# Two memory-key chunks inside the compression, and GpSimd in place of VectorE for the recurrence's resets

## The chip, the cores and the metric

One core of a Trainium2 chip runs the whole kernel. The metric is the device time of one execution in microseconds; lower is better. TensorE (PE), VectorE (DVE), ScalarE (ACT) and GpSimd (POOL) run their own instruction lists and meet only at semaphores; SyncE (SP) issues the weight transfers.

## The reference, cut to what matters

A decoder trunk of two layers over 512 tokens of width 1024. Layer 0 mixes with pooled channels and sparse attention, layer 1 with a gated linear recurrence (RG-LRU). Each layer then does cross-attention into 256 memory tokens and a gated FFN, with a layer norm after each part. The two pieces that the change touches:

```
# layer 0, sparse attention: 32 x 64 inputs of a block are compressed to one key and one value
blocks = raw[:, idx] + pos_emb[None, None, :, None, :]      # 31 blocks of 32 tokens
kc = rotary(blocks @ cmp_wk) ; vc = blocks @ cmp_wv
# layer 0, cross-attention: keys of the memory
kv = mem @ wkv ; k = kv[..., :D]
# layer 1, recurrence over the tokens, 1280 channels in 10 blocks of 128
r = sigmoid(xb @ wa + ba) ; i = sigmoid(xb @ wx + bx)
log_a = -8 * r * softplus(-lam)
a = exp(log_a) ; mult = sqrt(-expm1(2 * log_a))
reset = (positions == 0)
a = where(reset, 0, a) ; mult = where(reset, 1, mult)
h = scan(a, mult * (i * xc)) ; y = h * gelu(gate) ; out = y @ w_out
```

## The kernel before, in words

**Matrix products.** Every large product is done in three passes on TensorE: each operand is split into a rounded high part and a low remainder, and hi*hi, hi*lo and lo*hi are summed in PSUM (`passes`, L660). Weights come in chunks of 128 rows by 512 columns, through a ring of four buffers (`RING = 4`). A chunk c goes through four queues in this order:

1. SP issues the transfer into `w_raw`, once GpSimd has split chunk c-4 (`w_split`).
2. ACT rounds it into `w_hi` (`round_chunk`, L1111), once the transfer has landed and TensorE is done with chunk c-4 (`w_used`).
3. GpSimd subtracts to get `w_lo` (`split`, L623) and counts up `w_split`.
4. TensorE waits for `w_split` of chunk c, uses it, and counts up `w_used`.

GpSimd does nothing else after its first transfers: its list is `split` from the first chunk to the last, in order. Each engine's list is written out by hand. `PLAN` names groups of products, with their number of chunks and how many evacuations of PSUM ACT and DVE do for each. From it come the counts for which the engines wait (`ACT_BEFORE`, `DVE_AFTER` and so on), and the PSUM half: group i uses banks 0 to 3 or 4 to 7 in turn, and must wait for the evacuation of group i-2 (`begin`).

**Around the compression (layer 0).** TensorE does `tk` (transposes of the keys), then `cmp`: 128 small matmuls, a loop over 32 positions `l`, which the profile counts as 256 (L820). Then come chunks 0 to 3 of `k0_1` (memory keys, 8 chunks, 12 matmuls of 256 columns in each), `tkc` (transposes of the compressed keys), chunk 4, the compressed scores (L842, L845), chunk 5, `scores(0)` and `scores(1)`, chunks 6 and 7, `scores(2)`. `k0_1` lies in banks 4 to 7. The attention loop that follows transposes probabilities into banks 4 and 5 (`turn_probs`), sums outputs in bank 6 and memory values in bank 7, so it starts with `evacuated("k0_1")`: four copies by ACT (`keys_evac`, L1142), which stand behind `exps(0)`, `exps(1)` and three rounded chunks.

**The recurrence (layer 1).** The 10 channel blocks come in three sets, n = 0, 1, 2, of 4, 4 and 2. TensorE's order is `oin0`, `oin1`, the gates of set 0 (`ra0`, `ia0`; L967), `oin2`, the gates of set 1, `oin3`, the gates of set 2 (`ra2` holds both), `oin4`, then `oout0` and `oout1`. `oin4` reuses the banks of `oin3`, bank by bank, as ACT's gelu of `oin3` frees them. For each set ACT and DVE do in turn: sigmoid of r into `RA` (ACT, L1334), sigmoid of i (ACT, L1341), reset (DVE, L1758), tanh (ACT, L1350), two exponentials (ACT, L1354, L1356), `multipliers_squared` (DVE, L1786, L1788), square root (ACT, L1366), product and scan (`recurrence`, DVE, L1796, L1797), product with gelu (`y_tile`, DVE, L1804), rounding (`y_rounded`, ACT, L1304) and remainder (`y_low`, DVE). `conv` (DVE, L1768, L1771) makes the gates' input. ACT's rounding of weights is placed among these with `round_on(n, name)`. The reset works on r: `far` is 1e32 where the position is 0 and 0 elsewhere, so the maximum of r and `far` makes the decay 0 there.

Of the kernel before, what the change touches and what calls it, by code (L numbers as in the profile page):

```python
# [34 lines left out]
ALU = mybir.AluOpType  # L35
# [79 lines left out]
def plan_groups():  # L115


    g = [("x0", 0, 4, 4), ("x1", 0, 4, 4)]
    g += [("ein0", KT, 4, 0), ("tm", 0, 4, 4), ("ein1", KT, 4, 0), ("ein2", KT, 4, 0), ("ein3", KT, 4, 0)]
    g += [("mix", 0, 4, 4), ("k0_0", KT, 4, 0), ("tq0", 0, 2, 2), ("tq1", 0, 2, 2), ("tk", 0, 4, 4), ("cmp", 0, 2 + GROUP, 0), ("k0_1", KT, 4, 0), ("tkc", 0, 0, 0)]  # L120
    g += [(f"fv_{n}", KT, 1, 0) for n in range(D // FILL)]
    g += [("attn", 0, 0, 0)]
    g += [("eout0", KT, 0, 4), ("eout1", KT, 0, 4)]
    def norm(l, i, fillers=(None, None)):

        groups = [(f"ln{l}{i}_0", 0, 4, 4), (f"ln{l}{i}_1", 0, 4, 4)]
        return groups + [f for f in fillers if f]

    for l in range(DEPTH):
        if l:  # L130
            g += [("oin0", KT, 4, 0), ("oin1", KT, 4, 0), ("ra0", 0, 4, 0), ("ia0", 0, 4, 0)]
            g += [("oin2", KT, 4, 0), ("ra1", 0, 4, 0), ("ia1", 0, 4, 0)]
            g += [("oin3", KT, 4, 0), ("ra2", 0, 4, 0), ("oin4", KT, 4, 0)]
            g += [("oout0", RT, 0, 4), ("oout1", RT, 0, 4)]
            g += norm(1, 0)
        else:
            g += norm(0, 0)
        g += [(f"q{l}_0", KT, 4, 4), (f"q{l}_1", KT, 4, 4)]
        g += [(f"xo{l}_0", 0, 4, 4), (f"xo{l}_1", 0, 4, 4)]
        g += [(f"wo{l}_0", KT, 0, 4), (f"wo{l}_1", KT, 0, 4)]  # L140
        g += norm(l, 1) if l else norm(0, 1, (("k1_0", KT, 4, 0), ("k1_1", KT, 4, 0)))
        g += [(f"up{l}_{n}", KT, 2, 2) for n in range(FT // 2)]
        g += [(f"dn{l}_0", FT, 0, 4), (f"dn{l}_1", FT, 0, 4)]
        if l == 0:
            g += norm(0, 2, (("v1_0", KT, 2, 0), ("v1_1", KT, 2, 0)))
    return g
# [65 lines left out]
def hybrid_trunk(nc, a, out):  # L212

    ctx = ExitStack()
    with ctx:
# [149 lines left out]
        kc_ready = sem("kc_ready")  # L365
        scored, maxed, exped, turned = sem("scored"), sem("maxed"), sem("exped"), sem("turned")
        vc_cleared, cmp_scored, cmp_copied = sem("vc_cleared"), sem("cmp_scored"), sem("cmp_copied")
        weighted, copied_d, copied_a = sem("weighted"), sem("copied_d"), sem("copied_a")
        pv_done, o_hi_ready, o_ready = sem("pv_done"), sem("o_hi_ready"), sem("o_ready")

# [237 lines left out]
        @block.gpsimd  # L608
        def _(pool):

            for half in (0, 1):
                pool.dma_start(rows_posk[:, half, :], a["e_cmp_pos_k"][0]).then_inc(s_rows, 16)
                pool.dma_start(rows_posv[:, half, :], a["e_cmp_pos_v"][0]).then_inc(s_rows, 16)
            pool.dma_start(rows_ps[:, :], a["e_pool_scale"][0].rearrange("(g p) -> g p", p=P)).then_inc(s_rows, 16)
            pool.dma_start(rows_rg[0:CONV * RT, :], a["o_conv_w"][0].rearrange("n (j p) -> (n j) p", p=P)).then_inc(s_rows, 16)
            for n, name in enumerate(("o_conv_b", "o_ba", "o_bx", "o_lambda")):
                pool.dma_start(rows_rg[(CONV + n) * RT:(CONV + n + 1) * RT, :],
                               a[name][0].rearrange("(j p) -> j p", p=P)).then_inc(s_rows, 16)
            def split(first, last, m=0):
                for c in range(first, last):  # L620
                    (hi, lo), n = w_pair(c), WIDTH[c]
                    pool.wait_ge(w_rounded, c + 1 + RING * m)
                    nc.gpsimd.tensor_tensor(lo[:, :n], w_raw[:, c % RING, :n], hi[:, :n].bitcast(F32),  # L623
                                            ALU.subtract).then_inc(w_split, 1)

            done = 0
            for l in range(DEPTH):
                first, last = CHUNK0[f"up{l}_{UP_FIRST}"], CHUNK0[f"dn{l}_1"] + FT - HELD
                last = first + (last - first) // RING * RING
                split(done, first)  # L630
                with pool.Fori(0, (last - first) // RING) as m:
                    split(first, first + RING, m)
                done = last
            split(done, len(CHUNKS))


# [2 lines left out]
        def _(pe):  # L639
# [173 lines left out]
            pe.wait_ge(rawpos_ready, 4)  # L813
            pe.wait_ge(s_cmpw, 64)
            for l in range(CMP_BLOCK):
                for n in (0, 1):
                    for g in range(KV_HEADS):
                        half = slice(g * HD, (g + 1) * HD)
                        src = raw_pos[half, n, l // CMP_STRIDE, l:l + (NCMP - 1) * CMP_STRIDE + 1:CMP_STRIDE]
                        nc.tensor.matmul(ps[32 * n:32 * n + NCMP, b0 + g, 0:HD], src, cmp_w[half, n, l, :],  # L820
                                         start=(l == 0), stop=(l == CMP_BLOCK - 1))
            for t in range(TT):
                last = turn(ps[:, b0 + 2, t * GATES:(t + 1) * GATES], gateT[:, t * P:(t + 1) * P], GATES)
            last.then_inc(filled, 1)
            product("k0_1", mem, MEM, True, chunks=(0, KT // 2))
            b0 = begin("tkc")
            pe.wait_ge(kcdup_ready, 1)
            for g in range(KV_HEADS):
# [103 lines left out]
            product("k0_1", mem, MEM, True, chunks=(KT // 2 + 2, KT))  # L932
            pe.wait_ge(exped, 1)
            scores(2)
            evacuated("k0_1")
            for u in range(len(UNITS)):
                turn_probs(u)
                if u + 3 < len(UNITS):
                    pe.wait_ge(exped, u + 2)
                    scores(u + 3)  # L940
                for i in range(filled_until(u - 1), filled_until(u)):
                    memory_values(i)
                if u == len(UNITS) - 1:
                    evacuated("mix")
                    product("eout0", fm, SEQ, False, chunks=(0, 1), begun=True)
                weigh(u)
# [148 lines left out]
        def _(act):  # L1095
# [88 lines left out]
            filled_by("tk")  # L1184
            for j in range(4):
                nc.scalar.activation(kT_hi[:, j // 2, j % 2, :], bank("tk", j), ACT.Copy).then_inc(evac_a, 1)
            filled_by("cmp")
            b0 = 4 * (INDEX["cmp"] % 2)
            nc.scalar.activation(kc_tok[:, :, :], ps[0:NCMP, b0:b0 + 2, 0:HD], ACT.Copy).then_inc(evac_a, 1)
            act.wait_ge(vc_cleared, 2)  # L1190
# [34 lines left out]
            nc.scalar.activation(cmp_scores[:, 1, :], ps[:, 3, :], ACT.Copy).then_inc(cmp_copied, 1)  # L1225
            exps(0)
            exps(1)
            keys_evac(0, 1)
            for u in range(len(UNITS)):
                if UNITS[u][1] == "cmp" and u:  # L1230
                    output_hi(UNITS[u][0] - 1)
# [53 lines left out]
            for l in range(DEPTH):  # L1285
                if l:
# [74 lines left out]
                    def multipliers(n, meanwhile):  # L1361
                        done = sum(s[1] for s in RG_SETS[:n])
                        for j in range(RG_SETS[n][1]):
                            round_on(1 + (j == 0), meanwhile)
                            act.wait_ge(m2_ready, done + j + 1)
                            nc.scalar.activation(tm[:, j, :], tm[:, j, :], ACT.Sqrt).then_inc(mult_ready, 1)  # L1366


                    x_evac(0)
# [13 lines left out]
                    y_rounded(2, "oout0")  # L1383
                norm(l, 0)
                act.wait_ge(evac_a, ACT_BEFORE[f"q{l}_0"])
                for i in range(8):
                    if i < 4:
                        hi, full = k_hi[:, 2 * i:2 * i + 2, :], k_mem[:, 2 * i:2 * i + 2, :]
                    else:
                        m, n = (i - 4) // 2, i % 2  # L1390
                        hi, full = v_hi[:, m, 512 * n:512 * (n + 1)], v_mem[:, m, 512 * n:512 * (n + 1)]
                    nc.scalar.activation(hi, full, ACT.Copy).then_inc(kv_hi_ready, 1)
# [80 lines left out]
        def _(dve):  # L1473
# [186 lines left out]
            row_max(0)  # L1660
            row_max(1)
            weigh_probs(0)
            row_max(2)
            for u in range(len(UNITS)):
                turned_half(u)
# [71 lines left out]
            for l in range(DEPTH):  # L1737
# [5 lines left out]
                if l:  # L1743
# [5 lines left out]
                    dve.wait_ge(s_posb, 16)  # L1749

                    settle(nc.vector.tensor_copy(far[:, :], posb[:, :]))
                    settle(nc.vector.tensor_scalar(far[:, :], far[:, :], 0.0, FAR, ALU.is_equal, ALU.mult))

                    def resets(n):

                        for j in range(RG_SETS[n][1]):
                            dve.wait_ge(evac_a, ACT_BEFORE[f"ra{n}"] + j + 1)
                            nc.vector.tensor_tensor(RA[n][:, j, :], RA[n][:, j, :], far[:, :], ALU.max).then_inc(ra_reset, 1)  # L1758

                    def conv(n, part=None):  # L1760
                        first, tiles, name, b = RG_SETS[n]
# [49 lines left out]

                    conv(0)
                    conv(1, (0, 1))
                    resets(0)
                    conv(1, (2, 3))
                    multipliers_squared(0)
                    recurrence(0)
                    y_tile(0, 0)
                    y_tile(0, 1)
                    conv(2)  # L1820
                    resets(1)
                    multipliers_squared(1)
                    y_low(0, 0)
                    y_low(0, 1)
                    recurrence(1)
                    for j in range(4):
                        y_tile(1, j)
                    resets(2)
                    multipliers_squared(2)
                    for j in range(4):  # L1830
                        y_low(1, j)
                    y_tile(2, 2)
                    y_tile(2, 3)
                    recurrence(2)
                    y_low(2, 2)
                    y_tile(2, 0)
                    y_low(2, 3)
# [129 lines left out]
```

## Time and profile before

| what | value |
|---|---|
| median of 3 runs | 1492.19 us (1491.9 to 1496.13) |
| the profiled execution: its time, its span | 1492.09 us, 1490.3 us |
| PE / PE weight load busy | 98% / 82% |
| DVE / ACT / POOL busy | 38% / 41% / 45% |
| granted TensorE clock, mean | 0.999 of full speed |

The span runs from the first to the last instruction. The engines' shares are averages over the whole kernel, and the stages differ: between 855 and 960 us, where the recurrence is, DVE is busy for 90.31 of 105 us. A matmul of 512 columns is shown as 0.39 us long, but two of them start 0.23 us apart, since they overlap; idle time of PE is therefore read from the gaps that the timeline prints and not from busy shares alone.

### The profile page before, as it was taken

Reading aid. Unit: us, or ns where it says so; the run is one execution under the profiler, and the core shown is the slowest. Engines: PE = TensorE matmul, PEld = TensorE weight load, DVE = VectorE, ACT = ScalarE, POOL = GpSimd, SP = SyncE. Lnnn points to the kernel's source line nnn. Section 1 sums busy time; section 2 is a strip of 40 time slices with the busy share of each in tenths; the row PEclk is TensorE's granted clock in tenths of the full one; section 3 lists DMA queues with packets and bytes.
Section 4 is the critical chain, followed back from the end, with each engine's and each line's share of the span. In section 5 each row is a group of like instructions: output and inputs, shape, how many; then the busy total and the mean of one; then the engine's idle time right before and its main releaser. Section 6 shows DMA issues by size and latency. Waiting matters only on the chain.

```text
span 1490.3 us, 21214 instructions
## 1 busy us (share of the span) xinstructions
PE 1465.9 (98%) x7750; PEld 1227.7 (82%) x7750; DVE 559.5 (38%) x946; ACT 607.6 (41%) x1226; POOL 668.7 (45%) x530
## 2 busy tenths in 40 slices
PE   8999999999999999999999999999999999999998
PEld 7888888888888888888888867788888888888886
DVE  2753883833741101110123498664443101101014
ACT  3346764344343323332234397635433323323221
POOL 5543225233464454444457534543153454444442
PEclk9999999999999999999999999999999999999999
DMA  9332114221253333332234413323133333233222
GB/s 246 96 92 63 48 50 148 72 85 57 92 170 93 92 106 94 96 99 98 94 106 135 141 56 96 107 95 99 36 113 103 96 99 96 87 106 99 94 98 92
DMA packets 115713, 147.04 MB, mean 99 GB/s; under 512 B 20534, under 2 KB 74160, under 8 KB 115632
## 3 DMA queue, kind: packets, MB, share of 16 engines
q1 hardware_dynamic: 115312, 145.87, 32.2%
q8 instruction: 52, 0.85, 0.2%
q14 instruction: 29, 0.24, 0.1%
q0 software_dynamic: 320, 0.08, 0.0%
HBM read 143.80 MB, written 2.10 MB: 98 GB/s over the span
## 4 chain that ended last, share of the span: by engine, by line
PE 89%; DVE 4%; ACT 3%; issue 1%; POOL 1%; DMA 1%; SPq 0%; DVEq 0%; ACTq 0%
PE ps L660 81%; PE ps L665 4%; PE ps L914 1%; PE ps L868 1%; DVE h L1797 1%; POOL w_lo L623 1%; DVE h L1804 1%; DMA x_res<-in_x 1%; ACT w_hi L1111 0%; PE ps L967 0%; DVE h L1771 0%; ACT probs L1204 0%; ACT tm L1350 0%; DVE ib_alt L1788 0%; DVE ib L1796 0%
## 5 line engine op out<-in xcount | busy, mean ns | idle before, releaser
L623 POOL TENSOR_TENSOR w_lo<-w_raw,w_hi 128x512 fp32r<-128x512 f32 (+2 forms) x468 | 603.0, 1298 | 792.7 <-ACT w_hi L1111 791.0
L1111 ACT ACTIVATE w_hi<-w_raw 128x512 fp32r<-128x512 f32 (+2 forms) x468 | 279.6, 612 | 543.0 <-PE ps L660 521.7
L660 PE MATMUL ps<-fm_hi,w_hi 128*128 128x512 f32 (+1 forms) x1112 | 421.6, 379 | 4.1 <-POOL w_lo L623 3.0
L660 PE MATMUL ps<-fm_hi,w_lo 128*128 128x512 f32 (+1 forms) x1112 | 419.2, 377 | 0.0
L660 PE MATMUL ps<-fm_lo,w_hi 128*128 128x512 f32 (+1 forms) x1112 | 419.1, 377 | 0.0
L660 PEld LDWEIGHTS ps<-fm_hi,w_hi 128*128 128x128 f32 x1112 | 209.2, 188 | 45.8 <-POOL w_lo L623 4.6
L660 PEld LDWEIGHTS ps<-fm_hi,w_lo 128*128 128x128 f32 x1112 | 209.2, 188 | 38.6
L660 PEld LDWEIGHTS ps<-fm_lo,w_hi 128*128 128x128 f32 x1112 | 209.3, 188 | 38.1 <-issue 0.5
L1935 DVE TENSOR_TENSOR gf<-silu,ps 128x512 f32<-128x512 f32 x44 | 28.4, 685 | 418.8 <-ACT silu L1450 401.5
L1679 DVE SCALAR_TENSOR_TENSOR x_res<-x_res,ps 128x512 f32<-128x512 f32 x48 | 31.4, 685 | 273.5 <-PE ps L660 188.2
L660 PE MATMUL ps<-w_hi,g_hi 128*128 128x512 f32 x288 | 112.0, 389 | 0.0
L660 PE MATMUL ps<-w_hi,g_lo 128*128 128x512 f32 x288 | 112.0, 389 | 0.0
L660 PE MATMUL ps<-w_lo,g_hi 128*128 128x512 f32 x288 | 112.0, 389 | 0.0
L660 PEld LDWEIGHTS ps<-w_lo,g_hi 128*128 128x128 f32 x288 | 54.1, 188 | 11.3
L660 PEld LDWEIGHTS ps<-w_hi,g_lo 128*128 128x128 f32 x288 | 54.1, 188 | 11.2
L660 PEld LDWEIGHTS ps<-w_hi,g_hi 128*128 128x128 f32 x288 | 54.1, 188 | 11.1
L660 PE MATMUL ps<-w_hi,fm_hi 128*128 128x512 f32 x160 | 62.6, 391 | 0.4 <-ACT pool_in L1154 0.4
L660 PE MATMUL ps<-w_hi,fm_lo 128*128 128x512 f32 x160 | 62.3, 389 | 0.0
L660 PE MATMUL ps<-w_lo,fm_hi 128*128 128x512 f32 x160 | 62.3, 389 | 0.0
L1483 DVE TENSOR_TENSOR fm_lo<-ps,fm_hi 128x512 fp32r<-128x512 f32 x68 | 43.5, 684 | 23.7 <-ACT fm_hi L1137 13.7
L1263 ACT ACTIVATE lnc<-lnc 128x1 f32<-128x1 f32 x24 | 4.9, 204 | 94.8 <-DVE lnc L1719 94.8
L1137 ACT ACTIVATE fm_hi<-ps 128x512 fp32r<-128x512 f32 x48 | 26.1, 596 | 42.0 <-PE ps L665 41.6
(284 smaller groups left out, 2148.1 us busy)
## 6 DMA issues: line engine op xcount, KB each, us to landing
w_raw<-in_f_w_up SPq DMA_DIRECT2D x352, 128.0 KB, 2.1
w_raw<-in_f_w_down SPq DMA_DIRECT2D x88, 256.0 KB, 2.6
w_raw<-in_x_wkv SPq DMA_DIRECT2D x48, 256.0 KB, 3.1
w_raw<-in_o_w_in SPq DMA_DIRECT2D x40, 256.0 KB, 2.6
w_raw<-in_x_wq SPq DMA_DIRECT2D x32, 256.0 KB, 2.7
w_raw<-in_x_wo SPq DMA_DIRECT2D x32, 256.0 KB, 2.7
w_raw<-in_e_w_in SPq DMA_DIRECT2D x24, 256.0 KB, 3.3
w_raw<-in_o_w_out SPq DMA_DIRECT2D x20, 256.0 KB, 2.7
```

Of the source, the lines that this page charges most:

```text
L623: nc.gpsimd.tensor_tensor(lo[:, :n], w_raw[:, c % RING, :n], hi[:, :n].bitcast(F32), ALU.subtract).then_inc(w_split, 1)
L660: last = nc.tensor.matmul(outp, lhsT, rhs, start=(clear and k == 0 and n == 0), stop=(k == steps - 1 and n == 2), skip_group_check=True)
L665: return nc.tensor.transpose(out_, in_, ident[0:n, 0:n])
L868: last = nc.tensor.matmul(ps[:, b0 + hh % 2, c0:c0 + w], qT[:, hh, qb * P:(qb + 1) * P], k_[:, BRANCHES.index(b), hh // GROUP, :w], start= ...
L914: last = nc.tensor.matmul(quarter(ps[half, 6, cols]), kv_tok[:, kb, c0:c0 + HD], probsT[:, u % 2, turned_blocks, :], start=False, stop=(b ...
L1111: nc.scalar.activation(w_pair(c)[0][:, :n], w_raw[:, s, :n], ACT.Copy).then_inc(w_rounded, 1)
L1137: nc.scalar.activation(fm_target(hi, name, j), quarter(bank(name, j)), ACT.Copy).then_inc(evac_a, 1)
L1483: nc.vector.tensor_tensor(lo, full, hi.bitcast(F32), ALU.subtract).then_inc(done, 1)
L1679: nc.vector.scalar_tensor_tensor(out=xs, in0=xs, scalar=ALPHA, in1=bank(name, t), op0=ALU.mult, op1=ALU.add).then_inc(evac_d, 1)
L1797: nc.vector.tensor_tensor_scan(h[:, first + j, :], a_, i_, 0.0, ALU.mult, ALU.add).then_inc(h_ready, 1)
L1804: nc.vector.tensor_tensor(hj, hj, gelu[:, first + j, :], ALU.mult).then_inc(y_full, 1)
L1935: nc.vector.tensor_tensor(gf[:, j, :], silu[:, j, :], bank(name, 2 + j), ALU.mult).then_inc(evac_d, 1)
```

## The change

- `k0_1` begins inside the compression: its chunks 0 and 1 stand before position l = 24 of 32, chunks 2 and 3 after the compression.
- `k0_1` is evacuated by ACT (tiles 2, 3) and DVE (tiles 0, 1). TensorE waits only for DVE's two before the first `turn_probs`, and for ACT's two after it. ACT rounds two chunks of `k0_1` before it waits for `cmp`, and takes one of its three memory-value chunks before its copies, two after.
- The resets go from DVE to GpSimd, with add in place of maximum. GpSimd does the four, four and two of them after it has split the first chunk of `oin2`, `oin3` and `oin4`, each after a wait for ACT's sigmoid of that tile.
- In sets 1 and 2 ACT takes each square root ahead of the chunks that it rounds with it. In set 2 DVE does `recurrence(2)` ahead of `y_tile(2, 2)` and `y_tile(2, 3)`.

```diff
-... ("cmp", 0, 2 + GROUP, 0), ("k0_1", KT, 4, 0), ("tkc", 0, 0, 0)]
+... ("cmp", 0, 2 + GROUP, 0), ("k0_1", KT, 2, 2), ("tkc", 0, 0, 0)]
@@ gpsimd
                 done = last
+                if l == 0:
+                    for n, after in enumerate(("oin2", "oin3", "oin4")):
+                        split(done, CHUNK0[after] + 1)
+                        done = CHUNK0[after] + 1
+                        pool.wait_ge(far_ready, 1)
+                        for j in range(RG_SETS[n][1]):
+                            pool.wait_ge(evac_a, ACT_BEFORE[f"ra{n}"] + j + 1)
+                            nc.gpsimd.tensor_tensor(RA[n][:, j, :], RA[n][:, j, :], far[:, :], ALU.add).then_inc(ra_reset, 1)
             split(done, len(CHUNKS))
@@ tensor
             for l in range(CMP_BLOCK):
+                if l == 3 * CMP_BLOCK // 4:
+                    product("k0_1", mem, MEM, True, chunks=(0, 2))
...
-            product("k0_1", mem, MEM, True, chunks=(0, KT // 2))
+            product("k0_1", mem, MEM, True, chunks=(2, KT // 2))
...
-            evacuated("k0_1")
+            pe.wait_ge(evac_d, DVE_AFTER["k0_1"])
             for u in range(len(UNITS)):
                 turn_probs(u)
                 if u + 3 < len(UNITS):
                     pe.wait_ge(exped, u + 2)
                     scores(u + 3)
+                if u == 0:
+                    pe.wait_ge(evac_a, ACT_AFTER["k0_1"])
@@ scalar
-            filled_by("cmp")
+            round_weights(CHUNK0["k0_1"] + RING + 1)
+            group_filled(act, "cmp")
...
-            keys_evac(0, 1)
+            group_filled(act, "k0_1")
+            round_weights(CHUNK0["fv_0"] + 1)
+            for j in (2, 3):
+                nc.scalar.activation(k_mem[:, 4 + j, :], bank("k0_1", j)[:, :MEM], ACT.Copy).then_inc(evac_a, 1)
+            round_weights(CHUNK0["fv_0"] + RING - 1)
...
                         for j in range(RG_SETS[n][1]):
-                            round_on(1 + (j == 0), meanwhile)
+                            if n == 0:
+                                round_on(1 + (j == 0), meanwhile)
                             act.wait_ge(m2_ready, done + j + 1)
                             nc.scalar.activation(tm[:, j, :], tm[:, j, :], ACT.Sqrt).then_inc(mult_ready, 1)
+                            if n:
+                                round_on(1 + (j == 0), meanwhile)
@@ vector
             weigh_probs(0)
+            group_filled(dve, "k0_1")
+            for j in (0, 1):
+                nc.vector.tensor_copy(k_mem[:, 4 + j, :], bank("k0_1", j)[:, :MEM]).then_inc(evac_d, 1)
             row_max(2)
...
-                    def resets(n):
-
-                        for j in range(RG_SETS[n][1]):
-                            dve.wait_ge(evac_a, ACT_BEFORE[f"ra{n}"] + j + 1)
-                            nc.vector.tensor_tensor(RA[n][:, j, :], RA[n][:, j, :], far[:, :], ALU.max).then_inc(ra_reset, 1)
...
                     conv(1, (0, 1))
-                    resets(0)
                     conv(1, (2, 3))
...
-                    resets(1)
                     multipliers_squared(1)
...
-                    resets(2)
                     multipliers_squared(2)
                     for j in range(4):
                         y_low(1, j)
+                    recurrence(2)
                     y_tile(2, 2)
                     y_tile(2, 3)
-                    recurrence(2)
```

## Rows read from the trace of the kernel before

**Rows 1.** The page: busy shares, and the chain that ended last by engine.

```profile
PE 1465.9 (98%) x7750; PEld 1227.7 (82%) x7750; DVE 559.5 (38%) x946; ACT 607.6 (41%) x1226; POOL 668.7 (45%) x530
...
PE 89%; DVE 4%; ACT 3%; issue 1%; POOL 1%; DMA 1%; SPq 0%; DVEq 0%; ACTq 0%
```

**Rows 2.** Waits of PE, whole span: total us, times, longest us.

```profile
PE ps L660 <- POOL w_lo L623: 5.4, 9, 1.3
PE ps L820 <- issue: 1.6, 1, 1.6
PE ps L665 <- ACT k_mem L1142: 1.2, 1, 1.2
```

**Rows 3.** Window of the recurrence: length, busy PE, PEld, DVE, ACT, POOL.

```profile
855.00:960.00 105.00, 100.82 (x404) 75.23 (x403) 90.31 (x92) 84.59 (x131) 45.07 (x29) 1.00 0.27 81
```

**Rows 4.** Timeline of PE, recurrence: start, us, line, operation, [idle before, releaser].

```profile
864.09 0.79 PE L660 MATMUL ps<-fm_hi,w_hi 128*128 128x512 f32 x1
...
878.13 0.50 PE L660 MATMUL ps<-fm_hi,w_hi 128*128 128x512 f32 x1 [0.55 <-POOL w_lo L623]
...
893.58 0.79 PE L660 MATMUL ps<-fm_hi,w_hi 128*128 128x512 f32 x1
...
920.33 0.47 PE L660 MATMUL ps<-fm_hi,w_hi 128*128 128x512 f32 x1 [0.98 <-ACT gelu L1297]
...
935.35 0.50 PE L660 MATMUL ps<-fm_hi,w_hi 128*128 128x512 f32 x1 [1.13 <-POOL w_lo L623]
...
938.60 0.50 PE L660 MATMUL ps<-fm_hi,w_hi 128*128 128x512 f32 x1 [0.24 <-POOL w_lo L623]
...
959.21 0.50 PE L660 MATMUL ps<-w_hi,y_hi 128*128 128x512 f32 x1 [1.27 <-POOL w_lo L623]
```

**Rows 5.** Timeline of PE, compression and the start of the attention loop.

```profile
118.44 3.84 PE L820 MATMUL ps<-cmp_w,raw_pos 64*31 64x64 f32 x244
123.92 0.45 PE L820 MATMUL ps<-cmp_w,raw_pos 64*31 64x64 f32 x12 [1.64 <-issue]
...
148.69 0.39 PE L863 MATMUL ps<-causal_b,ident_b 128*128 128x256 bf16 x2 [0.19 <-ACT probs L1204]
```

**Rows 6.** Timeline of DVE, keys' remainder (evacuation of tk) and row_max(2).

```profile
119.18 2.48 DVE L1483 TENSOR_TENSOR kT_lo<-ps,kT_hi 128x512 fp32r<-128x512 f32 x4 [1.09 <-ACT kT_hi L1186]
...
143.95 1.22 DVE L1620 TENSOR_REDUCE negmax<-ps 128x8 f32<-128x1024 f32 x1 [2.78 <-PE ps L868]
```

**Rows 7.** Timeline of ACT, first operation of exps(2).

```profile
145.73 0.36 ACT L1204 ACTIVATE probs<-ps,negmax 128x128 f32<-128x128 f32 x1
```

**Rows 8.** Timeline of POOL, recurrence: one split, then merged runs of four and three.

```profile
853.15 1.29 POOL L623 TENSOR_TENSOR w_lo<-w_raw,w_hi 128x512 fp32r<-128x512 f32 x1 [1.19 <-ACT w_hi L1111]
...
888.51 7.02 POOL L623 TENSOR_TENSOR w_lo<-w_raw,w_hi 128x512 fp32r<-128x512 f32 x4 [10.43 <-ACT w_hi L1111]
...
913.81 5.01 POOL L623 TENSOR_TENSOR w_lo<-w_raw,w_hi 128x512 fp32r<-128x512 f32 x3 [2.70 <-ACT w_hi L1111]
```

**Rows 9.** Timeline of ACT, recurrence: one rounded chunk, and the sigmoids of r.

```profile
852.44 0.63 ACT L1111 ACTIVATE w_hi<-w_raw 128x512 fp32r<-128x512 f32 x1 [2.09 <-PE ps L660]
...
861.26 2.42 ACT L1334 ACTIVATE ra<-ps,chan 128x512 f32<-128x512 f32 x4
...
890.78 2.42 ACT L1334 ACTIVATE ra_alt<-ps,chan 128x512 f32<-128x512 f32 x4
...
922.97 1.27 ACT L1334 ACTIVATE ra<-ps,chan 128x512 f32<-128x512 f32 x2
```

**Rows 10.** Timeline of DVE: resets, and the same operation with and without POOL beside it.

```profile
864.15 3.59 DVE L1758 TENSOR_TENSOR ra<-ra,far 128x512 f32<-128x512 f32 x4
...
891.11 3.25 DVE L1804 TENSOR_TENSOR h<-h,gelu 128x512 f32<-128x512 f32 x2
...
947.86 1.29 DVE L1804 TENSOR_TENSOR h<-h,gelu 128x512 f32<-128x512 f32 x2 [0.75 <-ACT gelu L1297]
```

**Rows 11.** The page, DMA issues: KB each, us to landing.

```profile
w_raw<-in_o_w_in SPq DMA_DIRECT2D x40, 256.0 KB, 2.6
```

More of the change, by code:

```diff
@@ L119, in plan_groups @@
     g += [("ein0", KT, 4, 0), ("tm", 0, 4, 4), ("ein1", KT, 4, 0), ("ein2", KT, 4, 0), ("ein3", KT, 4, 0)]
-    g += [("mix", 0, 4, 4), ("k0_0", KT, 4, 0), ("tq0", 0, 2, 2), ("tq1", 0, 2, 2), ("tk", 0, 4, 4), ("cmp", 0, 2 + GROUP, 0), ("k0_1", KT, 4, 0), ("tkc", 0, 0, 0)]
+    g += [("mix", 0, 4, 4), ("k0_0", KT, 4, 0), ("tq0", 0, 2, 2), ("tq1", 0, 2, 2), ("tk", 0, 4, 4), ("cmp", 0, 2 + GROUP, 0), ("k0_1", KT, 2, 2), ("tkc", 0, 0, 0)]
     g += [(f"fv_{n}", KT, 1, 0) for n in range(D // FILL)]
@@ L367, in hybrid_trunk @@
         vc_cleared, cmp_scored, cmp_copied = sem("vc_cleared"), sem("cmp_scored"), sem("cmp_copied")
+        far_ready = sem("far_ready")
         weighted, copied_d, copied_a = sem("weighted"), sem("copied_d"), sem("copied_a")
@@ L1385, in _ @@
                 act.wait_ge(evac_a, ACT_BEFORE[f"q{l}_0"])
+                if l == 0:
+                    act.wait_ge(evac_d, DVE_AFTER["k0_1"])
                 for i in range(8):
@@ L1751, in _ @@
                     settle(nc.vector.tensor_copy(far[:, :], posb[:, :]))
-                    settle(nc.vector.tensor_scalar(far[:, :], far[:, :], 0.0, FAR, ALU.is_equal, ALU.mult))
-                    def resets(n):
-                        for j in range(RG_SETS[n][1]):
-                            dve.wait_ge(evac_a, ACT_BEFORE[f"ra{n}"] + j + 1)
-                            nc.vector.tensor_tensor(RA[n][:, j, :], RA[n][:, j, :], far[:, :], ALU.max).then_inc(ra_reset, 1)
+                    nc.vector.tensor_scalar(far[:, :], far[:, :], 0.0, FAR, ALU.is_equal, ALU.mult).then_inc(far_ready, 1)
                     def conv(n, part=None):
```

## The prediction

> **What bounds the kernel now.** I read the page first: PE is busy for 98% of the span and 89% of the chain that ended last is PE's [rows 1], so time is won or lost only where PE stands still. The waits of PE name those places: its waits for GpSimd's `w_lo` sum to 5.4 us over the whole kernel, one gap of 1.6 us in the compression is put down to "issue" (nothing that the profile shows), and one of 1.2 us is for the copies of `k_mem` [rows 2]. The window of the recurrence shows DVE busy for 90.31 and ACT for 84.59 of 105 us, and PE for 100.82 [rows 3]: DVE is crowded there, yet PE hardly waits. The timeline of PE shows what is to be had in that stage. Counting a gap as the distance of two starts less the usual 0.23 us, the printed idle times of 0.55, 1.13, 0.24 and 1.27 us are stalls of 0.7, 1.3, 0.4 and 1.4 us: 3.8 us together [rows 4]. No more can be won in the recurrence, however light DVE becomes. What matters instead is GpSimd: each 512-column chunk passes through it, and chunk 1 of `oin2` was split from 853.15 us, long before TensorE began `oin2` at 864.09 [rows 4, 8]. That lead is what the change spends.
>
> **The compression.** 244 of the 256 matmuls take 3.84 us (15.7 ns each), then comes the gap of 1.64 us, then the last 12 [rows 5]. The engine has its data, so I take the gap for instructions that don't arrive as fast as such small matmuls use them. The two chunks put in at l = 24 are 24 matmuls in about 2.9 us (0.12 us each); during them instructions can arrive, and the gap should go. l = 24 is reached after 192 matmuls, at 118.44 + 3.0 = 121.5; there `begin` now waits for the evacuation of `tk`, which DVE ends at 119.18 + 2.48 = 121.66 [rows 5, 6]: 0.2 to 0.3 us. Net gain 1.4 us. Chunks 0 and 1 of `k0_1` are split by then: ACT rounds up to chunk 2 of it before it evacuates `k0_0`. ACT's new rounds before `cmp` lie in 4 us in which it only waited.
>
> **The evacuation of k0_1.** PE waited 1.17 us for ACT's four copies. Now it needs two copies by DVE, which is idle for 2.78 us before `row_max(2)` [rows 6]; about 0.4 us each, they are hidden. But the wait doesn't vanish whole. `row_max(2)` needs `scores(2)`, so it still ends at 143.95 + 1.22 = 145.17, and `exps(2)`, which began at 145.73, can begin at 145.2 at best [rows 6, 7]. PE already waits 0.19 us for those exps at 148.69 [rows 5]. So some 0.5 us of the 1.2 stay as gain, between bounds of 0 and 1.2; without DVE's idle time the two copies would add 0.8 us to `row_max(2)`. This part and the last: 1.4 + 0.5 = 1.9 us gained, bounds 0 (the gap only moves) and 2.8.
>
> **The resets on GpSimd.** A reset is the same shape as a split, three 128x512 tiles in SBUF; alone a split takes 1.29 us [rows 8]. Beside a busy DVE it takes more: runs of four in 7.02 and three in 5.01 us are 1.75 and 1.67 each [rows 8]. DVE pays too: two `y_tile` products take 3.25 us with GpSimd beside them and 1.29 without, 1.0 us more each [rows 10]. DVE is busy at all three places, so I take 1.7 us, with 1.29 as the lower bound. Queued behind the resets on GpSimd are the splits, PE waits for those, and GpSimd can't start the resets before ACT's sigmoid, whatever lead it had. PE takes 2.72 us per chunk (ACT's rounding, released by PE, shows 2.09 idle + 0.63 [rows 9]); the first matmul after gates adds 0.4.
>
> - Set 0. First sigmoid done at 861.26 + 0.6 = 861.9 [rows 9]. Four resets and the split of chunk 1 of `oin2` are five operations: 861.9 + 8.5 = 870.4. PE wants that chunk at 864.09 + 0.4 + 2.72 = 867.2 [rows 4]. Stall 3.2 us (1.1 at 1.29).
> - Set 1. Sigmoid done at 891.4 [rows 9], chunk 1 of `oin3` split at 899.9, wanted at 893.58 + 3.1 = 896.7 [rows 4]. Stall 3.2 us (1.1). Sigmoid and PE are both later by then, by the same amount, as the gelus ahead of the sigmoid wait for PE's `oin2`.
> - Set 2. Sigmoid done at 922.97 + 0.65 = 923.6 [rows 9], two resets and a split, 5.1 us, chunk 1 of `oin4` at 928.7; wanted at 920.33 + 0.1 + 2.72 = 923.1 [rows 4]. Stall 5.6 us (4.4). Here even free resets would leave a stall, since the sigmoid comes too late.
>
> Sum 12.0 us (6.6). Transfers follow `w_split` too: chunk 5's is issued only when chunk 1 is split and lands 2.6 us later [rows 11], and ACT can round chunk 5 only when PE has used chunk 1, 2.7 us after the split. The two come together, so the transfer adds nothing, but ACT, and with it exps, roots and scans, now falls behind PE's delay; I count no second stall from it, as PE reaches chunk 5 another 8 us later. What a late PE takes back are the old stalls, whose causes (late rounds and late y tiles) had PE on time: 3.8 us. Net 12.0 - 3.8 = 8.2 us (2.8 at 1.29; 12.0 if none is given back).
>
> DVE loses its resets (3.59 us for the first four [rows 10]) but shares with ten resets and some three more splits at 1.0 us each: about even, and nobody waits for it in this stage once PE is late. ACT's roots ahead of rounds and `recurrence(2)` ahead of two y tiles bring results of DVE and ACT forward by 1 to 3 us, for a PE that comes 8 us late: cost and gain nothing; with PE on time they would be part of the 3.8.
>
> The Trainium skill (SBUF — State Buffer, section on who interferes with whom) says that a VectorE operation with two inputs in SBUF and a GpSimd operation that reads SBUF exclude each other for the whole instruction. By that, each reset could wait for a whole DVE operation, 1.9 us rather than the 1.7 of the rows, and the three stalls would be 15 us instead of 12.
>
> **The sum.** +8.2 - 1.9 = +6.3 us on the profiled execution's 1492.09, which is 0.1 below the median: 1498.5 us, slower by 0.42%.
>
> **Rivals.**
>
> - Within 0.3%: the resets run at 1.3 to 1.45 us, since DVE's convolution leaves GpSimd gaps. Net +2.8 to +4.5 in the recurrence, less 1.9: 1493 to 1495.5. For it: a lone split beside an idle DVE is 1.29. Against it: both long runs. 20%.
> - Faster: DVE is the real bound of the recurrence, its relief removes all old stalls, and no new one comes. 3.8 + 1.9 gives 1486.5 us. It needs five GpSimd operations between 861.9 and 867.2 us, under 1.06 each, and no row shows less than 1.29; in set 2 it can't be. 5%.
> - The clock falls: PE stands still for over 5 us in set 2. The granted clock was 1.00 throughout the stage [rows 3], with no gap beyond 1.3 us, so nothing before says what such a gap does. At 1.2 instead of 2.4 GHz a chunk takes 5.4 us; one to two such chunks add 2.7 to 5.4 us: 1501 to 1504. 12%.
> - The issue gap only moves to another place in the compression: 1500. 10%, part of the slower side.
>
> The Trainium skill (TensorE: Matmul & The Clock Gate, section on why this matters for kernels) warns that the clock drops to its lower level after idle gaps between matmuls; by it the third rival would be the likeliest for the longest gap. The waits before are too short to test it.
>
> **Numbers.** The forecast as it stands has 53%, which with the third and fourth rival makes 75% slower; 20% same, 5% faster. A difference under 0.3% (4.5 us) is what a measurement can't tell from none. Range: down to the low pace, up to the clock rival, 1493.5 to 1503.5.
>
> **What the profile after would show.** PE waits for POOL at chunk 1 of `oin2`, `oin3` and `oin4`, three gaps of about 3, 3 and 5.5 us, and none at `oout0`; resets on POOL at 1.5 to 1.8 us each; PE late by about 8 us at `oout0` less 2 us from the attention; compression without the 1.64 us gap; `turn_probs(0)` directly behind `scores(2)`. The prediction fails if chunk 1 is split in time after all, or if the three gaps feed further ones through ACT's rounds.

## The result, and the profile after

The changed kernel takes 1500.48 us (median of 4 runs, 1500.28 to 1502.19); the kernel before, timed beside it, 1492.05 us (1491.22 to 1496.13). The ratio is 1.0055, with a 95% interval of 1.0043 to 1.0067: 0.55% slower. The profiled execution took 1502.19 us, the slowest of the four; its span is 1500.4 us, 10.1 more than before.

The page and the waits of PE over the whole span of the changed kernel (times as in [rows 2]: total, count, longest):

```profile
PE 1472.5 (98%) x7750; PEld 1232.3 (82%) x7750; DVE 558.6 (37%) x938; ACT 607.8 (41%) x1224; POOL 683.8 (46%) x540
...
PE 93%; ACT 3%; POOL 2%; issue 1%; DVE 1%; DMA 0%; SPq 0%; DVEq 0%; ACTq 0%; POOLq 0%
```

```profile
PE ps L669 <- POOL w_lo L624: 11.9, 8, 3.6
PE ps L674 <- DMA x_res<-in_x: 5.3, 2, 5.0
PE ps L831 <- issue: 1.2, 1, 1.2
```

GpSimd's share rises by one point, and nothing but PE looks busy on the page; but PE's waits for `w_lo` have grown from 5.4 us [rows 2] to 11.9. The wait for `k_mem` is gone, the "issue" gap is not. DVE's part of the chain has shrunk from 4% [rows 1] to 1%: DVE was relieved, and the kernel is slower all the same.

The timeline of PE in the recurrence, to be read against [rows 4]:

```profile
868.49 0.80 PE L669 MATMUL ps<-fm_hi,w_hi 128*128 128x512 f32 x1 [2.96 <-POOL w_lo L624]
869.09 0.63 PE L669 MATMUL ps<-fm_lo,w_hi 128*128 128x512 f32 x1
869.51 0.63 PE L669 MATMUL ps<-fm_hi,w_lo 128*128 128x512 f32 x1
869.94 0.63 PE L669 MATMUL ps<-fm_hi,w_hi 128*128 128x512 f32 x1
...
882.41 0.50 PE L669 MATMUL ps<-fm_hi,w_hi 128*128 128x512 f32 x1 [0.55 <-POOL w_lo L624]
...
904.33 0.50 PE L669 MATMUL ps<-fm_hi,w_hi 128*128 128x512 f32 x1 [3.19 <-POOL w_lo L624]
...
935.06 0.50 PE L669 MATMUL ps<-fm_hi,w_hi 128*128 128x512 f32 x1 [3.62 <-POOL w_lo L624]
```

Three gaps stand at chunk 1 of `oin2`, `oin3` and `oin4`. By the distance of two starts less 0.23 us they are stalls of 3.1, 3.3 and 3.8 us. And behind the first one the matmuls start 0.43 us apart, not 0.23. The windows show why; the eighth value is the granted clock:

```profile
840.00:868.00 28.00, 25.54 (x98) 17.97 (x96) 20.24 (x18) 15.39 (x26) 18.05 (x11) 1.00 0.19 56
868.00:875.00 7.00, 6.51 (x16) 5.14 (x17) 6.86 (x6) 1.60 (x4) 5.43 (x5) 0.53 0.50 135
875.00:904.00 29.00, 25.60 (x98) 17.84 (x96) 24.73 (x25) 26.72 (x41) 14.33 (x9) 1.00 0.14 41
904.00:909.00 5.00, 4.67 (x13) 3.69 (x14) 0.00 (x0) 0.32 (x1) 3.98 (x4) 0.66 0.52 152
909.00:935.00 26.00, 22.44 (x92) 16.91 (x90) 22.24 (x22) 23.60 (x36) 10.11 (x8) 1.00 0.17 52
935.00:939.60 4.60, 4.54 (x13) 3.60 (x14) 0.56 (x1) 0.00 (x0) 4.18 (x4) 0.63 0.50 137
```

Around each gap the clock falls from 2.4 to 1.2 GHz. Counting matmuls that start 0.43 us apart, each 0.2 us late, gives 2.8, 1.5 and 1.5 us: 5.8 us in all. The first fall, with 14 such matmuls, is the odd one: the others have 8. In the profile of the recurrence part alone (below) all three falls are short, with 7 or 8 slow matmuls each.

The other side of the gaps is in GpSimd's timeline, next to [rows 8]:

```profile
860.25 6.52 POOL L642 TENSOR_TENSOR ra<-ra,far 128x512 f32<-128x512 f32 x4 [9.77 <-ACT ra L1352]
866.73 6.51 POOL L624 TENSOR_TENSOR w_lo<-w_raw,w_hi 128x512 fp32r<-128x512 f32 x4
...
895.88 6.72 POOL L642 TENSOR_TENSOR ra_alt<-ra_alt,far 128x512 f32<-128x512 f32 x4 [1.48 <-ACT ra_alt L1352]
902.55 5.43 POOL L624 TENSOR_TENSOR w_lo<-w_raw,w_hi 128x512 fp32r<-128x512 f32 x4
...
930.37 2.96 POOL L642 TENSOR_TENSOR ra<-ra,far 128x512 f32<-128x512 f32 x2 [9.85 <-ACT ra L1352]
```

GpSimd stands idle for 9.8 us at the head of its list, waiting for the first sigmoid, then does four resets in 6.5 us, and only then splits chunk 1, which needed nothing of all that.

The gates of set 0 start here, before and after:

```profile
857.62 7.03 PE L967 MATMUL ps<-h,w_gates 128*128 128x512 f32 x16
```

```profile
855.78 7.03 PE L980 MATMUL ps<-h,w_gates 128*128 128x512 f32 x16
```

The balance from there (1.84 us earlier than before) to the end of the span (10.1 later) is 11.9 us. The stalls are 10.2 and the half clock 5.8, together 16.0; given back are the old stalls of 1.3, 0.4 and 1.4 us and, with the wait for the gelu [rows 4], 1.2 us between the gates of set 2 and the second matmul of `oin4`: 4.3 together. The 0.7 us stall came back (at 882.41). 16.0 - 4.3 = 11.7. Of the 1.84 us ahead of the gates only 0.6 were won between the compression and the first scores of the attention loop; 0.3 lie ahead of 100 us and 1.1 between 410 and 425 us, around a wait of 0.64 us for `w_lo` at 420.11 that no edit touches and that most of the other profiles lack, too.

### The profile page after: what moved, and what is told of

Its sections match the earlier page's. It is cut to its first block, busy times and chain, and to the rows that moved or that the text cites. A ratio compares the mean times of both kernels' runs of the same rounds, so it can differ in the third digit from the quotient of the medians.

```text
span 1500.4 us, 21218 instructions
## 1 busy us (share of the span) xinstructions
PE 1472.5 (98%) x7750; PEld 1232.3 (82%) x7750; DVE 558.6 (37%) x938; ACT 607.8 (41%) x1224; POOL 683.8 (46%) x540
## 4 chain that ended last, share of the span: by engine, by line
PE 93%; ACT 3%; POOL 2%; issue 1%; DVE 1%; DMA 0%; SPq 0%; DVEq 0%; ACTq 0%; POOLq 0%
PE ps L669 86%; PE ps L674 4%; PE ps L925 1%; PE ps L879 1%; POOL w_lo L624 1%; POOL ra L642 1%; POOL ra_alt L642 0%; DMA x_res<-in_x 0%; ACT w_hi L1124 0%; PE ps L831 0%; ACT k_hi L1415 0%; ACT v_hi L1415 0%; PE ps L802 0%; PE ps L874 0%; ACT L1352 0%
```

## The experiments

The experiments ran in three groups. The runs of a group shared a chip and its runs of the kernel before, whose medians were 1492.07 us (lead three, fill, small resets, resets on DVE), 1492.62 (the attention part and its halves, the recurrence part) and 1492.8 (lead two, lead four, lead three with the old order). Ratios are to those. The change itself was timed apart from them, beside 1492.05 us.

**Lead of three: the resets one step further down.**

```diff
-                        split(done, CHUNK0[after] + 1)
-                        done = CHUNK0[after] + 1
+                        split(done, CHUNK0[after] + RING - 1)
+                        done = CHUNK0[after] + RING - 1
```

> The changed kernel with the resets one step further down GpSimd's list: behind the split of chunk 2 of oin2, oin3 and oin4 instead of chunk 0. The resets and everything else stay as they are. Theory (the cost is splits queued behind resets that wait for the sigmoid, and the clock that falls in the gaps they make): TensorE has three split chunks, 8 us of work, in hand while the resets run, so the three gaps of 3 to 4 us at chunk 1 go and the clock stays at full speed; the time falls by 10 to 12 us to 1488 to 1491. Rival (the cost is the resets' own work on GpSimd and the DVE operations that it holds up): ten resets are still there beside a busy DVE, so the time stays at 1498 to 1501.

Measured 1487.64 us, ratio 0.9967 (0.9955 to 0.9979). The resets are still there and take as long, but PE has three chunks in hand. In the window of 850 to 965 us PE waits for GpSimd twice, and GpSimd's timeline shows the same four operations in the same time:

```profile
PE ps L669 <- POOL w_lo L624: 1.1, 2, 0.8
```

```profile
859.37 6.54 POOL L642 TENSOR_TENSOR ra<-ra,far 128x512 f32<-128x512 f32 x4 [4.93 <-ACT ra L1352]
865.88 5.14 POOL L624 TENSOR_TENSOR w_lo<-w_raw,w_hi 128x512 fp32r<-128x512 f32 x3
...
891.85 6.85 POOL L642 TENSOR_TENSOR ra_alt<-ra_alt,far 128x512 f32<-128x512 f32 x4
```

So the resets' work costs nothing; their place in the list cost 12.8 us (1500.48 - 1487.64). The rival falls.

**Fill: useless work in the gaps.** TensorE uses chunk 0 of the three groups twice, so that chunk 0 counts twice in the output.

```diff
+                    if k == 0 and name in ("oin2", "oin3", "oin4"):
+                        for j in range(4):
+                            w = [w_[:, col0[j]:col0[j] + P] for w_ in w_pair(c)]
+                            last = passes(ps[:, b0 + j, :tokens], 1, steps, w, (hi[:, kk, :], lo[:, kk, :]), True)
                     last.then_inc(w_used, 1)
```

> The changed kernel, and TensorE uses chunk 0 of oin2, oin3 and oin4 a second time (48 matmuls in all three places together times three: 2.7 us of extra work in each gap), so that chunk 0 counts twice in the output. The gaps are filled with work that nobody needs; chunk 1 is split as late as before. Theory (the matmuls behind each gap run at half rate because the engine stood still): the granted clock stays at its upper level, the 0.43 us spacing goes, and the kernel gets FASTER with more work, by about 5 to 6 us, to 1494.5 to 1496. Rival (the slow matmuls are slow for another reason, such as GpSimd's or ACT's traffic in the same stretch): 0.43 us spacing stays and the time is 1500 to 1503.

Measured 1495.86 us, ratio 1.0025 (1.0015 to 1.0034): 4.6 us faster than the change, with 8.2 us more matmuls (three times 12 of 0.227 us). PE's waits for GpSimd from 850 to 970 us, and windows:

```profile
PE ps L669 <- POOL w_lo L624: 1.6, 4, 0.9
```

```profile
855.00:885.00 30.00, 29.54 (x115) 21.17 (x114) 27.04 (x25) 23.93 (x38) 17.44 (x11) 1.00 0.23 62
885.00:915.00 30.00, 29.83 (x118) 21.73 (x117) 26.96 (x24) 25.75 (x40) 19.00 (x13) 1.00 0.26 71
915.00:945.00 30.00, 29.06 (x122) 22.40 (x121) 23.70 (x22) 22.49 (x35) 16.01 (x11) 1.00 0.33 105
```

The clock is 1.00 in every window. From each set's gates to the next set's, GpSimd is busy for 17.8 and 19.2 us in the changed kernel and for 17.4 and 20.1 here, ACT for 27.8 and 26.4 and for 27.8 and 26.6, DVE for 31.1 and 24.1 and for 30.9 and 28.8; the bursts of transfers behind chunk 1 are here, too (DMA share 0.48 from 901.5 to 906 us and 0.64 from 931 to 936, at a clock of 1.00). So it is the standing still of TensorE that lowered the clock. The fill is 8.2 us above lead three, which is just its extra work. That parts the loss of 12.8 us against lead three in two: some 8.2 of standing still and 4.6 of half clock, each good to some 1.5 us, as the medians' intervals are.

**Small resets: waiting without the work.** Only columns 0 to 7 of each tile get their reset.

```diff
-nc.gpsimd.tensor_tensor(RA[n][:, j, :], RA[n][:, j, :], far[:, :], ALU.add)
+nc.gpsimd.tensor_tensor(RA[n][:, j, 0:8], RA[n][:, j, 0:8], far[:, 0:8], ALU.add)
```

> The changed kernel with each reset cut to the first 8 of 512 columns (only columns 0 to 7 get their reset; the waits and the order stay). It parts the waiting for the sigmoid from the resets' work. Theory: in sets 0 and 1 the sigmoid alone is early enough (the last of four sigmoids ends 3 us before TensorE wants chunk 1), so no gap there; in set 2 a gap of up to 1 us is left, since the second sigmoid ends 0.5 us before chunk 1 is wanted and the split takes 1.3 to 1.7 us. Clock full. Time 1487 to 1490. Rival (the wait at the head of GpSimd's list costs by itself, work or not): gaps of over 2 us stay in all sets, time over 1495.

Measured 1488.32 us, ratio 0.9972 (0.9963 to 0.9981). PE's timeline has these two gaps in the recurrence, the first at the old place late in `oin2`, the second at chunk 1 of `oin4`:

```profile
876.77 0.50 PE L669 MATMUL ps<-fm_hi,w_hi 128*128 128x512 f32 x1 [0.64 <-POOL w_lo L624]
...
922.51 0.50 PE L669 MATMUL ps<-fm_hi,w_hi 128*128 128x512 f32 x1 [1.80 <-POOL w_lo L624]
```

As forecast, set 2 keeps a gap even with almost no reset work, since the sigmoid itself comes too late; at 1.8 us it is larger than the 1 us expected. In sets 0 and 1 it was the resets' length, on top of the wait for the sigmoid, that made chunk 1 late. The clock stays up after 1.8 us.

**Lead of two, and of four.** The same two lines with `CHUNK0[after] + 2` and `CHUNK0[after] + RING`.

> The changed kernel with the resets behind the split of chunk 1 of oin2, oin3 and oin4 (lead of two chunks; the change has one, the run with lead three took 1487.6). Theory (TensorE's lead in split chunks decides): the resets and the next split end 2.7 us earlier against TensorE's need, so gaps of 0.3 to 1.1 us stay where there were 3.1 to 3.8, all too short to make the clock fall: 1488.5 to 1491. Rival (a clock that falls after any gap there): 1493 to 1496.

Measured 1491.74 us, ratio 0.9992 (0.9983 to 1.0001), 0.7 us above what was expected: PE waits 4.5 us for GpSimd in this stage, where 0.3 to 1.1 us per set was forecast. The two largest gaps in PE's timeline are in `oin3` and `oin4`:

```profile
901.46 0.50 PE L669 MATMUL ps<-fm_hi,w_hi 128*128 128x512 f32 x1 [1.82 <-POOL w_lo L624]
...
928.92 0.50 PE L669 MATMUL ps<-fm_hi,w_hi 128*128 128x512 f32 x1 [1.95 <-POOL w_lo L624]
```

The clock stays at 1.00 here too.

> The changed kernel with the resets behind the split of chunk 3 (lead of four). Now the resets come later than they could: chunk 3 is rounded by ACT behind the sigmoids, so each set's resets, and ACT's tanh behind them, come 1.7 us later than with lead three. Theory: TensorE's gaps at the chunk behind the resets are gone, but ACT waits longer for resets and passes it on to its rounds: 1487.5 to 1490.5, not better than lead three. Rival (more lead is better still): under 1487.

Measured 1490.38 us, ratio 0.9984 (0.9975 to 0.9993). The waits of ACT between 850 and 970 us show the other side of the trade:

```profile
ACT tm L1368 <- POOL ra L642: 5.1, 5, 1.6
ACT tm L1368 <- POOL ra_alt L642: 2.7, 3, 1.0
```

With lead three ACT's tanh waits 0.4 and 1.9 us at these two; here 5.1 and 2.7. PE waits 3.4 us in this stage, on chunks that ACT rounds late. By lead the times are 1500.5, 1491.7, 1487.6 and 1490.4 us: three is best. These times come from three groups of runs, and the intervals of three and four just touch (0.9979 and 0.9975). The traces say the same of the stage by itself: from the start of the gates of set 0 to the end of the span it is 632.7 us before, 644.6 with the change, 633.2 with lead two, 629.5 with three (630.5 with three and the old order) and 631.8 with four.

**Resets back on DVE, all else of the change kept.** The loop in GpSimd's list goes, and `resets(n)` with `ALU.max` stands where it stood before.

> The changed kernel with the resets back on DVE, where they were, and back as maximum; everything else of the change stays (k0_1 in the compression, its shared evacuation, roots ahead of rounds in sets 1 and 2, recurrence(2) ahead of two y tiles). Theory: all that was lost came with the resets' move, so the time goes below that of the kernel before: 0.5 to 2 us by the attention part and 0.5 to 2 us by the new order in the recurrence (the 1.4 us gap at oout0): 1488.5 to 1491. Rival (the new order of ACT or DVE costs something too): 1493 or more.

Measured 1491.18 us, ratio 0.9989 (0.998 to 0.9998): 0.1% faster, just above the expected range. Its profile is 1.5 us ahead of the kernel before when the recurrence begins and 0.9 us ahead at the second half of `oout1`, so the new order alone gained nothing there. The whole loss lies in the resets' move. This run and lead three differ only in the resets and were timed in one group: with the resets off DVE and out of the way of the splits the kernel is 3.5 us faster.

**Lead three with the old order.** Square roots behind the rounds in all sets, two y tiles ahead of `recurrence(2)`.

> Lead three with the old order of the roots (behind the rounds in all sets) and of set 2 (two y tiles ahead of the recurrence). With the resets on DVE the new order brought nothing that shows in the recurrence. Theory: the gain of lead three over the attention part alone (1489.9) comes from the resets having left DVE, and the order adds at most 1 us: 1487.5 to 1489. Rival (the new order is what pays, once DVE is relieved): 1489.5 or more.

Measured 1488.16 us, ratio 0.9971 (0.9959 to 0.9983), against 0.9967 with the new order: no difference that can be told. So the gain over resets on DVE is that of the resets having left it.

**The attention part, whole and in its two halves.**

> The kernel before with the attention part of the change alone: chunks 0 and 1 of k0_1 inside the compression, and the shared evacuation of k0_1. By the prediction 1.9 us faster, 1490.2. By the profile after, where the issue gap came back elsewhere in the compression (1.18 us) and the first scores of the loop came 0.6 us earlier than before once an earlier start is taken off: 0.6 us faster, 1491.4.

> The kernel before with chunks 0 and 1 of k0_1 inside the compression and nothing else. By the prediction (the gap is instructions that don't keep up, and the two chunks give them time) 1.4 us faster, 1490.7. Rival (the gap only moves to another matmul of the compression, as in the profile after): no change, 1492, with a gap of 1 to 1.7 us at L820 in the profile.

> The kernel before with the shared evacuation of k0_1 and nothing else. By the prediction 0.5 us faster, 1491.6, because the exps behind row_max(2) set the next scores; if row_max(2) were no limit, 1.2 us, 1490.9.

> The changed kernel with the attention part undone: only the recurrence part of the change. Theory: the whole loss is here, so 1500.5 plus what the attention part gained, 1501 to 1502.5. Rival (the attention part, too, adds to the loss): under 1500.

The diffs are those of the change, cut to the edits of `k0_1`: chunks 0 and 1 inside the compression with ACT's earlier rounds (compression only), the two copies on DVE with the waits that go with them (evacuation only), both (attention only), and all but these (recurrence only). Measured: attention only 1489.92 us, ratio 0.9984 (0.9975 to 0.9993); compression only 1490.82 us, 0.9988 (0.9979 to 0.9997); evacuation only 1492.35 us, 0.9996 (0.9987 to 1.0005); recurrence only 1502.84 us, 1.0063 (1.0049 to 1.0076). So the attention part gains 0.16%, some 2.4 us, most of it from the compression; the evacuation's 0.3 us can't be told from nothing by the medians; and the recurrence part alone (1502.84, 0.3 us above the expected range) is as much slower than the whole change (1500.48).

In the profile of the recurrence part alone, PE's three gaps are these, and the clock fell at each of them:

```profile
870.97 0.50 PE L669 MATMUL ps<-fm_hi,w_hi 128*128 128x512 f32 x1 [2.95 <-POOL w_lo L624]
...
904.90 0.50 PE L669 MATMUL ps<-fm_hi,w_hi 128*128 128x512 f32 x1 [2.79 <-POOL w_lo L624]
...
935.93 0.50 PE L669 MATMUL ps<-fm_hi,w_hi 128*128 128x512 f32 x1 [3.90 <-POOL w_lo L624]
```

What the medians can't tell of the evacuation the traces can. Measured against the kernel before at the same matmuls, all ten kernels with the shared evacuation gain 0.5 us between 143 and 150 us, and the two without it (compression only, recurrence only) nothing. That is the forecast 0.5: the wait of 1.2 us for `k_mem` is gone, and the scores behind it come only half as much earlier.

```profile
145.08 0.44 PE L665 MATMUL ps<-consts,probs 128*128 128x128 f32 x2 [1.17 <-ACT k_mem L1142]
```

```profile
147.78 0.39 PE L874 MATMUL ps<-causal_b,ident_b 128*128 128x256 bf16 x2
```

The first line is of the kernel before. The second, of the changed kernel, is the same matmul as the one at 148.69 in [rows 5]: 0.9 us earlier, of which 0.4 were won ahead of it.

How the compression gains is less simple than the prediction had it. Its timeline in the changed kernel:

```profile
118.15 1.96 PE L831 MATMUL ps<-cmp_w,raw_pos 64*31 64x64 f32 x116
121.29 1.40 PE L831 MATMUL ps<-cmp_w,raw_pos 64*31 64x64 f32 x76 [1.18 <-issue]
125.67 1.19 PE L831 MATMUL ps<-cmp_w,raw_pos 64*31 64x64 f32 x64
```

With attention only:

```profile
118.48 3.14 PE L822 MATMUL ps<-cmp_w,raw_pos 64*31 64x64 f32 x192
124.85 1.19 PE L822 MATMUL ps<-cmp_w,raw_pos 64*31 64x64 f32 x64
```

With evacuation only (the compression as before), timeline and windows:

```profile
118.30 1.96 PE L820 MATMUL ps<-cmp_w,raw_pos 64*31 64x64 f32 x116
121.39 2.09 PE L820 MATMUL ps<-cmp_w,raw_pos 64*31 64x64 f32 x128 [1.13 <-issue]
124.86 0.45 PE L820 MATMUL ps<-cmp_w,raw_pos 64*31 64x64 f32 x12 [1.37 <-issue]
```

```profile
118.00:127.00 9.00, 6.50 (x272) 5.95 (x271) 3.90 (x14) 3.27 (x9) 0.00 (x0) 0.94 0.02 5
127.00:131.00 4.00, 4.00 (x26) 4.00 (x26) 0.19 (x2) 2.17 (x5) 2.53 (x2) 0.70 0.13 30
```

The gap can stand behind matmul 116, behind 244, at both, or at neither. Of the ten profiles with the chunks inside (the changed kernel and nine experiments), none has the one behind 244, six have one behind 116 (1.1 to 1.5 us), which lies ahead of the inserted chunks, and four have none. The four are 1.3 us ahead of the kernel before across the compression, as forecast; the six are within 0.2 us of it. The compression-only profile is one of the six and is only 0.5 us ahead of the kernel before, though its median is 1.8 us ahead; so one profile of each says little of this part. Without the chunks there are three profiles, each with the gap behind 244, and in two of them (evacuation only, recurrence only) the clock also fell right behind the compression, to 0.70 and 0.72 in windows of 4 and 6 us; with the chunks inside it never did. In the recurrence-only profile that cost 1.5 us between the compression and `tkc`. So the median gain of 1.8 us is one over a mixture: a gap that is sometimes there, and a fall of the clock that was seen only without the chunks.

## Why the prediction was right, and where not

The forecast of 1498.5 us and slower by 0.42% met 1500.48 and 0.55%, inside the range. The main mechanism held; that the sum came as near as 2 us is in part luck, since the clock was left out of it and set 2 was too large.

- **Splits queued behind the resets.** Right: gaps at the three places named, of 3.1, 3.3 and 3.8 us against 3.2, 3.2 and 5.6. Resets ran at 1.63, 1.68 and 1.48 us each; 1.7 was taken. Lead three shows the cause by taking it away. By the rule of the Trainium skill (SBUF — State Buffer, who interferes with whom) the prediction worked out 1.9 us per reset, more than the mean of any of the three runs: on average a reset didn't wait for a whole DVE operation.
- **Set 2 was too large**, 5.6 for 3.8. The term that was off is the place where PE would want chunk 1. It was read from a TensorE that had waited 0.98 us for the gelu [rows 4], with the sigmoid 0.5 us later. In the changed kernel PE was late and ACT less so: no gelu wait, and the sigmoid's first tile was done near 930.2, before chunk 1 was wanted at 931.3. From the first reset at 930.37 to TensorE's start at 935.06 the two resets (2.96 us) and one split take 4.7 us, and the stall is 3.8.
- **Old stalls given back.** 3.8 us were forecast; 3.1 of them went, the 0.7 us one came back at 882.41, since ACT's rounds are held up with PE, and 1.2 us at the gelu went instead. Sum 4.3: right in size, by other parts.
- **The clock.** This is the step that failed. The forecast kept the clock at full speed and gave its fall 12%, only in set 2, for "over 5 us". It fell at all three gaps, of 3.0 to 3.6 us of idle time, and cost 4.6 us by the fill (5.8 by counting matmuls in the one profile, whose first fall was a long one). In the recurrence-only profile it fell at all three, too, of 2.95, 2.79 and 3.90 us. The rule of the Trainium skill (TensorE: Matmul & The Clock Gate, why this matters for kernels) that idle gaps bring the clock down was right here, and the trace before had no gap in the recurrence beyond 1.3 us to show it; it deserved more than 12%. The 1.8 us too much in set 2 and the 4.6 to 5.8 us of half clock that were not in the sum partly cancelled.
- **DVE's relief.** Worth nothing in the change, as forecast. But it was a part of the 3.8 us to be had with PE on time, and lead three took it: 1487.64 us against 1491.18 with the resets on DVE, in one group (and against 1489.92 for the attention part alone, in another).
- **Attention.** 1.9 us were forecast and 2.4 measured for the part alone. The sizes of the halves were 1.4 and 0.5; by the medians they came out as 1.8 and 0.3, the second inside its uncertainty; by the traces the second is 0.5, and the first 1.3 where no gap stood. That the gap would go because instructions get time fits the gap behind matmul 244; the one behind 116 lies ahead of the chunks and stays, so the fourth rival (a gap at another place) describes the changed kernel's profile, with a gain of 0.1 us across the compression. The two places lie 128 matmuls apart, with as many weight loads between them, which suits instructions that come in blocks; what the gaps are was not shown.
- **A sum of the first rival.** Its +4.5 us, less 1.9, is 1494.8 us and not 1495.5. Nothing else rests on it.

## What to carry to other kernels

Work that moves to a less busy engine moves into its list. Ask first what that list feeds, how far it runs ahead, and put the moved work, with its wait, behind as many items as its consumer needs to live through it: here the same ten operations cost some 10 us with a lead of one chunk and gained 2 to 3.5 with a lead of three, and a lead of four made the other consumer wait. A gap of 3 us on TensorE can cost more than 3 us, because the clock falls with it: in this kernel each such gap cost about half as much again, and gaps of up to 2 us cost only themselves.

## What the runs showed of the hardware

- The granted TensorE clock went from 2.4 to 1.2 GHz around gaps of 2.96, 3.19 and 3.62 us in the changed kernel and of 2.95, 2.79 and 3.90 us in the recurrence part alone, and stayed at 2.4 after gaps of up to 1.95 us, in all profiles of the recurrence. No gap between 1.95 and 2.79 us occurred. Useless matmuls in the gap kept it up and made the kernel 4.6 us faster than without them.
- It also fell behind the compression, whose matmuls are 64x64 with 31 rows and 16 ns apart, in two of three profiles without memory-key chunks inside it, one with a gap of 1.36 us, one with two of 1.13 and 1.37 us; the third, the kernel before, had the longest gap, 1.64 us, and no fall, so the gap's length doesn't decide it there. With the chunks inside it fell in none of ten.
- A 128x512 GpSimd operation of 1.29 us alone [rows 8] took 1.48 to 1.75 us each in the runs of resets and splits beside a busy DVE, and an operation of DVE of 0.65 us took 1.6 beside it [rows 10].
